# A fused block of four mixers and an expert layer on one NeuronCore: the scan's transposes, GpSimd's pauses and the order of cross attention's output rearranged

## The chip, the cores and the metric

The kernel runs on one core of one Trainium2 chip. It is a single program for a batch of one sequence of 512 tokens with 1024 features, in float32. The metric is the time of one execution on the device in microseconds (us). A core has five engines with queues of their own: PE (matrix multiplications and transposes), DVE (vector work), ACT (activations and scaled copies), POOL (GpSimd: elementwise work, and here the issue of the gathers) and SP (issue of DMAs). They meet only through semaphores.

## The reference, cut to what matters

```python
def peer(h, p):                                   # the expert layer, after cross attention
    q = h @ p["peer_wq"]                          # 8 heads x 2 halves of 128
    s = einsum(q, p["peer_sub_keys"])             # 128 scores for each half
    a, b = top_k(s[first half], 16), top_k(s[second half], 16)
    best, ids = top_k(a[:, None] + b[None, :], 16)      # of 256 sums; id = i * 128 + j
    gates = softmax(best)                         # per head
    u, v = p["peer_u"][ids], p["peer_v"][ids]     # 16 rows of each for a token and head
    return sum(gates * gelu(u . h) * v)
x = x + rmsnorm(mamba2(rmsnorm(x)))               # state space mixer, scan over 4 chunks
x = x + rmsnorm(window_attention(rmsnorm(x)))
x = x + gated_delta_net_and_mlstm(rmsnorm(x))
x = x + cross_attention(rmsnorm(x), memory) @ w_o
x = rmsnorm(x + peer(rmsnorm(x)))
```

(Names are shortened. Every token of the expert layer needs 8 x 16 rows of a table of 16384 rows; `peer_u` and `peer_v` lie beside each other in it, so a row is 8 KB.)

## The kernel before, in words

The 512 tokens are four tiles of 128 (`TT = 4`), and 1024 features are eight blocks of 128 (`DT = 8`). The residual stream `resid` stays on the chip from the first stage to the last.

**Weights.** All dense weights are one stream of units of 128 x 1024. SP loads them into a ring of four (L188). POOL splits each into a high and a low part (`split_weights`, L208 and L211; `split_ahead`, L227 and L229), and PE multiplies in three passes (high x high, high x low, low x high) from two buffers `w_parts`. `w_split` counts split units, and `w_used` the units that PE is done with; a unit may be split when the one two before it has been used. In a product to token tiles (`tokens_out`, L281) a unit serves 4 tiles with 24 matmuls, and 4 units make a chunk of 512 output features.

**Start.** `set_up` issues the four quarters of x, the table of columns, and the first four weight units, and waits for the columns; only after the barrier at its end may `mamba_in` transpose x (L432).

**State space scan.** `mamba_scan` turns 24 blocks of 128 features (96 transposes, L840) through four PSUM banks. DVE copies the even blocks out (L856) and ACT the odd ones (L882). ACT computes the softplus of the time steps after its first four copies (L888 to L891), with two table loads; PE sums the decays only behind the last transpose (L844, L846); then ACT and DVE make the exponentials (L894 to L898, L870, L872), and a barrier follows.

**Output projections.** `NormedOut` (twice: after the scan and after window attention) multiplies by the output weights, scales (L553), sums (L555), adds into `resid` tile by tile (L563), and PE transposes each tile as it is added (L432). The next projection's units are split meanwhile.

**mLSTM.** In `mlstm` DVE works through four chunks (L2378 to L2385), each signalled by `mixed_ready`; POOL multiplies the gate in (L2206) when its chunk is signalled, and scales later (L2209). ACT squares each chunk (L2152) for the norm.

**Cross output and expert layer** (`peer`). `PlainOut` makes chunk 0 and chunk 1 of cross attention's output for all four tiles, adds them (L498), and turns blocks 0 to 3 between the units of chunk 1 and blocks 4 to 7 after it. Then PE computes the queries of the first two columns x = 0, 1 in two halves (L2811: tiles 0 and 1 are "front", 2 and 3 "back", 24 matmuls with 256 columns for each), their scores (L2822), the columns 2 and 3 for all tiles (L2850), and their scores (L2859). DVE picks the best sixteen (`vector_top`, L2665 to L2672), combines two halves of a head and writes the ids (`Choice.vector`, L2730 to L2750). The choice of head 0 is made for tile 0 first, so that gathers can begin, then tile 1. `Choice.vector_gates` needs ACT's exponentials (`Choice.scalar`, L2766). In ACT's queue those of tile 1 stand behind the scores of column 2.

The experts are 512 gathers, each of 128 rows of 8 KB (1.05 MB), issued by POOL (L3078) in a fixed order. Nine buffers are there until gather 207, then thirteen; a gather waits until the row before it in its buffer has been used (`row_used`). For each pair of rows DVE makes the dot products (L3101), ACT the gelu (L3139), DVE the weight (L3093), ACT a diagonal matrix (L3135), and PE adds the weighted rows into PSUM (L3156, four matmul records for a row). Splits of the columns 4 to 15 stand between the gathers in POOL's queue; the first stands ahead of gather 15.

## Time and profile before

| | us |
|---|---|
| median of 3 runs (lowest, highest) | 2681.82 (2678.59, 2682.61) |
| the profiled execution: its own time, and its span | 2678.74, 2677.0 |
| PE busy (share of the span) | 2320.1 (87%) |
| DVE busy | 1568.4 (59%) |
| POOL busy | 1502.8 (56%) |
| ACT busy | 714.9 (27%) |
| DMA queue of the gathers: share of 16 engines' time | 48.3% |

The page of the profile has busy time by engine, the span in 40 slices, and the chain of work that ended last. A share of busy time is a mean over stages with different limits, so the table alone does not say what a change in one stage is worth.

### The profile page before, as it was taken

The numbers are of one execution on the slowest core, as the hardware profiler recorded it, in microseconds if no ns is written. First come the engines' busy times: TensorE is split into PE (matmuls) and PEld (weight loads), VectorE is DVE, ScalarE is ACT, GpSimd is POOL, SyncE is SP. The second block draws the span as 40 slices with busy tenths as digits, with TensorE's granted clock in tenths as the row PEclk, the third lists the DMA queues.
The fourth block names the chain that finished last, engine by engine and source line by source line (L and its number), as shares of the span: only waits on it lengthen the run. The fifth ranks groups of instructions, "written<-read, shape, count | busy, mean of one in ns | idle before, by whom it ended". The sixth has DMA issues, their size and how long they took to land.

```text
span 2677.0 us, 28363 instructions
## 1 busy us (share of the span) xinstructions
PE 2320.1 (87%) x9216; PEld 1519.9 (57%) x9216; DVE 1568.4 (59%) x3381; ACT 714.9 (27%) x1935; POOL 1502.8 (56%) x1060
## 2 busy tenths in 40 slices
PE   8999899899989999789988888888777777777776
PEld 7888678788978879677754443444232223222222
DVE  1266592333431668632387878887778776555555
ACT  2111553214422131423222222222223222111112
POOL 7777377676567754264665656555544444344331
PEclk9999899999989999899999999999999999999999
DMA  4222002222222210031289999999999999999996
GB/s 146 93 95 94 17 1 93 91 100 80 103 88 87 86 63 1 1 110 48 100 339 408 421 421 421 421 413 421 421 422 422 421 421 422 421 422 421 421 421 258
DMA packets 105898, 646.35 MB, mean 241 GB/s; under 512 B 12720, under 2 KB 15152, under 8 KB 39600
## 3 DMA queue, kind: packets, MB, share of 16 engines
q0 software_dynamic: 73728, 536.90, 48.3%
q1 hardware_dynamic: 31776, 106.87, 11.6%
q8 instruction: 65, 1.06, 0.2%
q10 hardware_dynamic: 272, 1.05, 0.1%
q14 instruction: 57, 0.47, 0.0%
HBM read 640.58 MB, written 4.19 MB: 241 GB/s over the span
## 4 chain that ended last, share of the span: by engine, by line
DMA 32%; PE 10%; DVE 5%; POOL 2%; issue 1%; ACT 1%; POOLq 0%; DVEq 0%; ACTq 0%
DMA peer_row<-in_peer_uv,peer_ids 32%; PE bank L3156 7%; DVE peer_row L3101 3%; PE bank L281 2%; POOL peer_row L3078 1%; PE bank L2850 1%; POOL w_parts L229 1%; ACT peer_diag L3135 1%; DVE peer_weight L3093 1%; PE bank L2811 0%; POOL w_parts L227 0%; DVE peer_top_i L2669 0%; DVE peer_picked L2742 0%; DVE peer_sc_left L2672 0%; DVE peer_top_v L2665 0%
## 5 line engine op out<-in xcount | busy, mean ns | idle before, releaser
L3156 PE MATMUL bank<-peer_row,peer_diag 128*128 128x512 f32 x2048 | 966.8, 618 | 266.7 <-ACT peer_diag L3135 264.5
L3078 POOL DMA_INDIRECT peer_row<-in_peer_uv,peer_ids x512 | 585.8, 1144 | 645.6 <-PE bank L3156 604.4
L3156 PEld LDWEIGHTS bank<-peer_row,peer_diag 128*128 128x128 f32 x2048 | 380.0, 194 | 823.5 <-ACT peer_diag L3135 430.0
L3101 DVE CUSTOM_DVE_ANT_0 peer_row<-peer_row,peer_h_tok 128x1024 f32<-128x1024 f32 x512 | 641.0, 1256 | 329.2 <-DMA peer_row<-in_peer_uv,peer_ids 328.3
L208 POOL TENSOR_TENSOR w_parts<-ring,zero 128x1024 fp32r<-128x1024 f32 x156 | 295.5, 1894 | 227.5 <-PE bank L281 112.4
L211 POOL TENSOR_TENSOR w_parts<-ring,w_parts 128x1024 fp32r<-128x1024 f32 x156 | 374.4, 2400 | 29.0 <-POOL w_parts L208 29.0
L3139 ACT ACTIVATE peer_acts<-peer_dots 128x2 f32<-128x2 f32 x256 | 52.1, 204 | 734.0 <-DVE peer_dots L3101 734.0
L3135 ACT ACTIVATE peer_diag<-ident,peer_weight 128x128 f32<-128x128 f32 x512 | 177.5, 394 | 223.8 <-DVE peer_weight L3093 221.1
L257 PE MATMUL bank<-ssm_h_high,w_parts 128*128 128x512 f32 x512 | 157.7, 389 | 0.8 <-DVEq L644 0.8
L257 PEld LDWEIGHTS bank<-ssm_h_high,w_parts 128*128 128x128 f32 x512 | 96.1, 188 | 20.9 <-DVEq L644 1.0
L257 PE MATMUL bank<-hyb_h_high,w_parts 128*128 128x512 f32 x320 | 99.9, 393 | 0.8 <-DVEq L644 0.8
L281 PE MATMUL bank<-w_parts,att_h_high 128*128 128x512 f32 x320 | 98.9, 390 | 1.7 <-DVE att_h_low L442 1.5
L257 PE MATMUL bank<-ssm_h_low,w_parts 128*128 128x512 f32 x256 | 99.6, 389 | 0.0
L2850 PE MATMUL bank<-peer_h_high,w_parts 128*128 128x512 f32 x192 | 86.8, 493 | 0.0
L281 PE MATMUL bank<-w_parts,ssm_h_high 128*128 128x512 f32 x256 | 78.9, 389 | 0.0
L281 PE MATMUL bank<-w_parts,ssm_y_high 128*128 128x512 f32 x256 | 78.8, 389 | 0.0
L3093 DVE TENSOR_TENSOR peer_weight<-peer_acts,peer_gates 128x2 f32<-128x2 f32 x256 | 51.9, 203 | 35.1 <-ACT peer_acts L3139 26.6
L227 POOL TENSOR_TENSOR w_parts<-ring,zero 128x1024 fp32r<-128x1024 f32 x22 | 42.6, 1935 | 49.4 <-ACT xa_p L2573 34.1
L257 PEld LDWEIGHTS bank<-hyb_h_high,w_parts 128*128 128x128 f32 x320 | 60.9, 190 | 13.8 <-DVEq L644 1.0
L281 PEld LDWEIGHTS bank<-w_parts,att_h_high 128*128 128x128 f32 x320 | 59.8, 188 | 14.6 <-issue 1.8
L229 POOL TENSOR_TENSOR w_parts<-ring,w_parts 128x1024 fp32r<-128x1024 f32 x22 | 62.9, 2858 | 1.7
L672 ACT ACTIVATE ssm_conved<-ssm_acc 128x512 f32 x32 | 20.2, 632 | 161.6 <-DVE ssm_acc L661 161.6
(559 smaller groups left out, 3803.8 us busy)
## 6 DMA issues: line engine op xcount, KB each, us to landing
ring<-in_weights SPq DMA_DIRECT2D x180, 512.0 KB, 3.2
peer_row<-in_peer_uv,peer_ids POOLq DMA_INDIRECT x512, 25.4
resid<-in_x SPq DMA_DIRECT2D x4, 512.0 KB, 7.6
out<-resid SPq DMA_DIRECT2D x4, 512.0 KB
xa_mem<-in_mem ACTq DMA_DIRECT2D x1, 1024.0 KB, 4.9
xa_kept<-xa_v_out SPq DMA_DIRECT2D x1, 1024.0 KB
xa_kept<-xa_k_out SPq DMA_DIRECT2D x1, 1024.0 KB
xa_v<-xa_kept SPq DMA_DIRECT2D x1, 1024.0 KB, 5.3
```

The lines of the kernel that those rows point to most:

```text
L208: pool.tensor_tensor(high, m.ring[:, s, :], zeros, ALU.add).then_inc(m.w_high, 1)
L211: pool.tensor_tensor(low, m.ring[:, s, :], high, ALU.subtract).then_inc(m.w_split, 1)
L229: pool.tensor_tensor(low, m.ring[:, u % RING, :], high, ALU.subtract).then_inc(m.w_split, 1)
L257: mm = pe.matmul(out, m.parts[:, s % 2, a, k * P:(k + 1) * P], rhs[b][:, k, :], start=(k == 0 and (a, b) == PASSES[0]), stop=(k == DT - 1 ...
L281: mm = pe.matmul(bank_of(c, t)[:, :], lhs[a][:, k, t * P:(t + 1) * P], m.parts[:, u % 2, b, (k % 2) * 512:(k % 2 + 1) * 512], start=(k == ...
L2850: mm = pe.matmul(self.q_bank(x)[:, :], parts[:, x % 2, a, k * P:(k + 1) * P], self.h[b][:, k, :], start=(k == 0 and (a, b) == PASSES[0]), ...
L3078: pool.indirect_dma_start(self.rows[row][:, :], None, self.m.ins["peer_uv"], bass.IndirectOffsetOnAxis(ap=self.choice.ids[:, t, slot:slot ...
L3093: dve.tensor_tensor(self.weight[:, g % 4, :], self.acts[:, g % 4, :], self.choice.gates[:, t, first:first + GROUP], ALU.mult).then_inc(sel ...
L3101: dot = dve.tensor_tensor_reduce(mine, mine, self.tokens(slot_of(j)[0]), 1.0, 0.0, ALU.mult, ALU.add, self.dots[:, h % 4, r:r + 1])
L3135: act.activation(self.diag[:, j % (2 * GROUP), :], self.m.ident[:, :], ACT.Copy, scale=self.weight[:, g % 4, r:r + 1]).then_inc(self.diag_ ...
L3139: act.activation(self.acts[:, h % 4, :], self.dots[:, h % 4, :], ACT.Gelu).then_inc(self.acts_ready, 1)
L3156: mm = pe.matmul(self.m.banks[2 * t + half][:, :], self.diag[:, j % (2 * GROUP), :], self.rows[row][:, D + half * 512:D + (half + 1) * 512 ...
```

## The change

It edits six places.

1. `set_up` issues only the first quarter of x and the columns and waits for nothing; the other loads are issued at the head of `mamba_in`, and ACT waits for the columns there. The three small rows of `mamba_scan` are loaded in `mamba_in` too.
2. `mamba_scan` turns its blocks through seven banks. DVE takes blocks 0 to 3 and the even ones, ACT the other odd ones. The time steps' chain comes first on DVE and ACT, the sums stand behind block 13, and the exponentials among the last copies.
3. and 4. In the two stages with `NormedOut`, POOL makes the high part of the next projection's first unit, and then pauses until all four tiles have been added. In the second, the small weights are split four units later.
5. In `mlstm`, POOL's gate product of chunk t waits for chunk t + 1.
6. In `peer`, chunk 1 of cross output is made for tiles 0 and 1 first. Four pairs of split weights are held for it. Then come unit 0 of chunk 1 for tiles 2 and 3, the front's transposes, queries and scores, the other three units for tiles 2 and 3, and the back half. The norm is made for each pair of tiles. On DVE the sums of tiles 2 and 3 come after the first choice. Places in memory are changed to fit: the first gather waits until all of cross output's units are used (its buffer lies where the left operand lay), gather 6 until both back halves are done, and gather 8 for the two token tiles.

```diff
@@ split_ahead
+        if pause is not None and u == m.split:
+            pool.wait_ge(*pause)
         pool.tensor_tensor(low, m.ring[:, u % RING, :], high, ALU.subtract).then_inc(m.w_split, 1)
@@ set_up
-            for n in range(4):
-                here = slice(n * D // 4, (n + 1) * D // 4)
-                sp.dma_start(m.resid[:, :, here], x[:, :, here]).then_inc(m.x_loaded[n], 16)
-                if n == 0:
-                    sp.dma_start(m.cols[:, :], m.ins["cols"]).then_inc(loaded, 16)
-                    sp.dma_start(m.ring[:, 0, :], m.ins["weights"][0]).then_inc(m.w_loaded[0], 16)
-            stream_weights(m, sp, RING)
-            sp.wait_ge(loaded, 16)
+            load_tokens(m, sp, 0)
+            sp.dma_start(m.cols[:, :], m.ins["cols"]).then_inc(m.cols_loaded, 16)
@@ mamba_scan
+            SUMS_AFTER, EXPS_AFTER = 13, 15
+            turn_banks = [m.banks[n] for n in (0, 1, 2, 3, 5, 6, 7)]
+            dve_takes = lambda j: j < 4 or j % 2 == 0
                 for j in range(N_TURN):
...
+                    if j == SUMS_AFTER:
+                        pe.wait_ge(dve_dt, 3)
...
@@ mamba_out_attention_in, attention_out_hybrid_in
+            split_ahead(m, pool, RING, pause=(out.added, TT))
@@ HeadNorm.gpsimd
-        pool.wait_ge(self.mixed_ready, t + 1)
+        pool.wait_ge(self.mixed_ready, t + 2)
@@ PairOut (new)
+    def tensor_front(self, pe):
+        for kk in range(4):
+            self.tensor_unit(pe, 0, kk, range(TT))
+        for kk in range(4):
+            self.tensor_unit(pe, 1, kk, (0, 1))
+            if kk < 2:
+                pe.wait_ge(self.added, TT)
+                for k in (2 * kk, 2 * kk + 1):
+                    for t in range(TT):
+                        self.turn.tensor(pe, k, t)
+    def tensor_turn(self, pe, pair):
+        for k in range(4, DT):
+            if k == 4:
+                pe.wait_ge(self.added, TT + 2 * pair + 2)
...
@@ peer, gpsimd
+            out.gpsimd(pool)
+            for x in range(2):
+                queries.gpsimd_split(pool, x, queries.parts, None)
+            for x in range(2, FIRST):
+                queries.gpsimd_split(pool, x, m.parts, queries.u0 - 4 + x - 1)
...
+                if j == 0:
+                    pool.wait_ge(m.w_used, queries.u0)
+                if j == 6:
+                    pool.wait_ge(m.w_used, queries.u0 + 2)
+                if j == 8:
                     pool.wait_ge(tokens_made, 2)
@@ peer, tensor
+            out.tensor_front(pe)
             m.unit += HP
...
+            out.tensor_unit(pe, 1, 0, (2, 3))
+            out.tensor_turn(pe, 0)
+            for x in range(2):
+                queries.tensor_half(pe, x, 0)
+            for x in range(2):
+                queries.tensor_half_scores(pe, x, 0)
+            for kk in range(1, 4):
+                out.tensor_unit(pe, 1, kk, (2, 3))
+            pe.wait_ge(queries.front_read, 2)
+            out.tensor_turn(pe, 1)
...
@@ peer, scalar
             choice.scalar(act, 0, 0, 0, 1)
+            out.scalar_pair(act, 1)
+            for x in range(2):
+                queries.scalar_half_q(act, x, 1)
+            for x in range(2):
+                queries.scalar_half_scores(act, x, 1)
             queries.scalar_q(act, 2)
             queries.scalar_q(act, 3)
             queries.scalar_scores(act, 2)
@@ peer, vector
+            out.vector_first(dve)
+            out.vector_pair(dve, step, 0)
...
             choice.vector(dve, step, 0, 0, 1, alone)
+            for t in range(2, TT):
+                out.add(dve, 1, t)
             dve.wait_ge(gain_loaded, 16)
             dve.wait_ge(rms.ready, 1)
             tokens(0, alone)
+            out.vector_rest(dve, step, 1)
```

## Rows read from the trace of the kernel before

**Rows 1.** The page: DMA share in 40 slices, in tenths, and GB/s.

```profile
DMA  4222002222222210031289999999999999999996
GB/s 146 93 95 94 17 1 93 91 100 80 103 88 87 86 63 1 1 110 48 100 339 408 421 421 421 421 413 421 421 422 422 421 421 422 421 422 421 421 421 258
```

**Rows 2.** Windows: stretch, busy us (and count) by engine, PEclk, DMA share, GB/s.

```profile
1352.00:1353.00 1.00, 1.00 (x7) 0.81 (x6) 1.00 (x2) 0.00 (x0) 1.00 (x1) 1.00 0.00 0
1355.00:1356.00 1.00, 1.00 (x6) 0.83 (x5) 0.88 (x5) 0.00 (x0) 0.70 (x2) 1.00 0.94 385
...
1550.00:1600.00 50.00, 44.47 (x122) 21.71 (x121) 40.69 (x104) 13.85 (x42) 29.74 (x22) 1.00 1.01 421
```

**Rows 3.** Timeline of the start, PE: start, us, engine, line, operation, [idle before].

```profile
9.52 5.21 PE L432 MATMUL bank<-ident,resid 128*128 128x128 f32 x24 [0.90 <-DMA resid<-in_x]
14.48 0.71 PE L281 MATMUL bank<-w_parts,ssm_h_high 128*128 128x512 f32 x2
```

**Rows 4.** Timeline of the scan's transposes: PE, ACT and DVE.

```profile
297.00 6.69 PE L840 MATMUL bank<-ident,ssm_conved 128*128 128x128 f32 x44 [2.68 <-ACT ssm_xs L882]
...
292.66 0.30 ACT L888 ACTIVATE ssm_tmp<-ssm_dt 128x128 f32<-128x128 f32 x1
...
296.36 1.07 ACT L882 ACTIVATE ssm_xs<-bank 128x512 f32<-128x512 f32 x2
...
306.94 0.29 DVE L872 TENSOR_TENSOR ssm_dt_end<-ssm_dt,ssm_dt_end 128x128 f32<-128x128 f32 x1 [0.38 <-ACT ssm_dt_end L898]
```

**Rows 5.** The line L563, first output projection: duration in ns, least, median, most.

```profile
L563 DVE SCALAR_TENSOR_TENSOR resid<-ssm_z_gate,ssm_o_stat,resid x4: 1271/1272/2900, 502.1 to 507.3; 128x1024 f32<-128x1024 f32 x4
```

**Rows 6.** Timeline after the first output projection: POOL and PE.

```profile
501.56 2.34 POOL L211 TENSOR_TENSOR w_parts<-ring,w_parts 128x1024 fp32r<-128x1024 f32 x1 [0.18 <-POOL w_parts L208]
...
505.03 5.80 PE L432 MATMUL bank<-ident,resid 128*128 128x128 f32 x32 [5.73 <-DVE resid L563]
...
512.38 0.70 PE L281 MATMUL bank<-w_parts,att_h_high 128*128 128x512 f32 x2 [1.55 <-DVE att_h_low L442]
```

**Rows 7.** Timeline of mLSTM's end: DVE.

```profile
1131.87 0.16 DVE L2384 TENSOR_TENSOR mls_den<-mls_den,mls_weights 128x4 f32<-128x4 f32 x1
...
1135.47 1.10 DVE L2384 TENSOR_TENSOR mls_den<-mls_den,mls_weights 128x4 f32<-128x4 f32 x1
```

**Rows 8.** The chain that ended last, around the first choice: start, us, what.

```profile
1341.18 5.75 PE bank L2811 x48
...
1348.11 10.91 PE bank L2850 x48
1359.03 2.91 PE bank L2859 x16
...
1364.14 1.22 DVE peer_row L3101
```

**Rows 9.** Timeline, DVE and POOL: the first choice and the gathers 0, 9 and 15.

```profile
1341.21 0.29 DVE L2665 MAX8 peer_top_v<-peer_sc_front 128x8 f32<-128x128 f32 x1 [2.86 <-ACT peer_sc_front L2838]
...
1351.27 1.93 POOL L3078 DMA_INDIRECT peer_row<-in_peer_uv,peer_ids  x1 [6.54 <-DVE peer_ids L2750]
...
1372.83 1.41 POOL L3078 DMA_INDIRECT peer_row<-in_peer_uv,peer_ids  x1 [9.63 <-PE bank L3156]
...
1388.94 1.76 POOL L3078 DMA_INDIRECT peer_row<-in_peer_uv,peer_ids  x1
```

**Rows 10.** Timeline, PE and ACT: column scores, then the first rows.

```profile
1358.87 2.01 PE L2859 MATMUL bank<-peer_keys,peer_q 128*128 128x128 f32 x16
1368.77 11.76 PE L3156 MATMUL bank<-peer_row,peer_diag 128*128 128x512 f32 x22 [7.90 <-ACT peer_diag L3135]
...
1361.96 0.63 ACT L2876 ACTIVATE peer_sc_front<-bank,peer_norm_stat 128x128 f32<-128x128 f32 x2 [2.30 <-PE bank L2859]
...
1364.88 0.63 ACT L2876 ACTIVATE peer_sc_front<-bank,peer_norm_stat 128x128 f32<-128x128 f32 x2 [1.25 <-remote]
```

**Rows 11.** A window around the first rows of the experts, the columns as in rows 2.

```profile
1366.10:1372.90 6.80, 4.13 (x5) 1.85 (x6) 6.28 (x25) 3.02 (x7) 0.07 (x1) 0.50 1.02 428
```

More of the change, by code:

```diff
@@ L217, in split_weights, with split_ahead @@
         four(i, u0, False)
-def split_ahead(m, pool, n, parts=None):
+def split_ahead(m, pool, n, parts=None, pause=None):
     for u in range(m.split, m.split + n):
@@ L782, in _ @@
         def _(act):
+            act.wait_ge(m.cols_loaded, 16)
             for k in range(DT):
@@ L2789, in __init__, with gpsimd_split @@
         self.u0 = m.unit + DT
-        self.parts = m.at(58, "peer_parts", [P, 2, 2, UNIT], F32R)
+        self.parts = m.at(74, "peer_parts", [P, 2, 2, UNIT], F32R)
+    def gpsimd_split(self, pool, x, parts, used):
+        m, u = self.m, self.u0 + x
+        high, low = (parts[:, x % 2, n, :] for n in range(2))
+        pool.wait_ge(m.w_loaded[u % RING], 16 * (u // RING + 1))
+        if used is not None:
+            pool.wait_ge(m.w_used, used)
+        pool.tensor_tensor(high, m.ring[:, u % RING, :], m.zero[:, :].broadcast_to([P, UNIT]), ALU.add).then_inc(m.w_high, 1)
+        pool.wait_ge(m.w_high, u + 1)
+        pool.tensor_tensor(low, m.ring[:, u % RING, :], high, ALU.subtract).then_inc(m.w_split, 1)
+        m.split += 1
     def q_bank(self, x):
```

238 lines of the change are left out of this document (165 added, 73 removed).

## The prediction

> **What bounds the kernel now.** I read the page first, for where the DMA engines are full. From slice 20 on they move 408 to 422 GB/s [rows 1], and a stretch in the middle of the experts shows 1.01 of their time busy with PE at 44.47 of 50 us [rows 2]. That is a hard floor: 512 gathers of 1.05 MB at 421 GB/s are 2.49 us each, 1275 us, and no engine's saving shortens them. So the time has two parts. Ahead of the first gather it is set by PE and by the handovers at which PE waits; there a microsecond saved is a microsecond. Behind it, it is set by when the stream of gathers begins to flow and whether it ever dries up. I then read the timelines at each place that the diff touches [rows 3 to 7], the chain of waits across the first choice [rows 8], and the timeline of the gathers [rows 9].
>
> How the stream begins decides the last part. The first gather is issued at 1351.27 [rows 9]; in 1352 to 1353 nothing moves, in 1355 to 1356 it is 385 GB/s [rows 2], and a ramp between them puts the first bytes at about 1353.9, so 2.6 us after the issue. Nine buffers hold nine gathers, which last until 1353.9 + about 0.7 (ramp) + 9 x 2.49 = 1377.0. The tenth can be issued only when PE has used the first row: 1372.83, bytes from 1375.4. So the stream survives with 1.6 us to spare. An earlier first gather is worth its gain only if the tenth comes earlier too.
>
> **Start: 0.** PE's quarter-one transposes begin at 9.52 on the arrival of x, and the first product at 14.48 [rows 3]. The barrier that falls away let PE begin earlier, but the later quarters come in the same saturated byte stream, the last blocks still wait for them, and their issues now stand behind the barrier. I take 0; from 1.5 gained (the first quarter's blocks out of the way) to 1.0 lost (the issues of one load after another, later).
>
> **Scan: -6.4.** Before, PE waits 2.68 us for a bank [rows 4], since ACT makes the softplus from 292.66 on and takes a bank out only from 296.36, 3.7 us. Behind the last transpose (297.00 + 6.69 = 303.7) come sums, exponentials and table load until 306.94 + 0.29 = 307.23, a tail of 3.5. After, seven banks with DVE on blocks 0 to 3 cover the softplus, and the tail's work lies beside transposes 13 to 23. Walking the 96 transposes at 0.15 us each (6.69 / 44) with the copies at 0.54 (1.07 / 2) dealt between two engines, the last copy ends at about 300.85 instead of 307.23: 2.68 less in the stall, 3.5 less in the tail and 0.2 in the copies. Range -7.5 to -4.5: the lower end if a bank is short once for some 2 us.
>
> **Pauses: -4.1.** The first of four L563 takes 2.900 us, the others 1.27 [rows 5]. POOL's low part runs from 501.56 for 2.34 us [rows 6], so to 503.90; the add began at 502.1 and ends 1.27 behind 503.7 at 505.0, where PE's wait of 5.73 us ends. With the pause that add takes 1.27: 1.63 less. The small reduction ahead of it, which stands beside POOL's high part, gives about 0.4 more (an estimate: the small operation in [rows 7] shows 1.10 beside POOL and 0.16 alone). So 2.05; the second projection has the same pattern once more (its first add at 792.1), so 4.1 in all. What the pause costs: the low part now begins after the four adds, about 4.5 us later, and each unit behind it comes about that much later. PE needs it at about 510.4 (512.38 less 2.0 [rows 6]) and it would be done at about 509.2; the cover is PE's 5.80 us of transposes and the split of that one block in DVE and ACT. If that cover were gone, up to 1 us comes back: range -4.8 to -3.0.
>
> The Trainium skill, page "SBUF — State Buffer", section "Who interferes with whom", says that a DVE instruction with two SBUF inputs and a GpSimd instruction that reads SBUF share one port pair, and that the first to issue holds it for its whole length. The trace agrees (2.900 beside 1.27). By that rule the change also pays somewhere: it moves the splits of columns 0 to 2 beside the first choice, where DVE's pair sums read SBUF twice.
>
> **mLSTM: -0.5.** L2384 takes 1.10 beside POOL's product and 0.16 alone [rows 7]; in two of the chunks' steps it is on the way. But the product moved a chunk later stands beside other small operations. From -1.3 to +0.3.
>
> **Peer: +4.5.** Ahead of the choice PE no longer makes three units of chunk 1 for tiles 2 and 3. These are 3 x 12 matmuls at 0.227 (10.91 / 48 [rows 8]), 8.2; blocks 4 to 7 of two tiles, 8 transposes at 0.15, 1.2; and about 0.6 for a norm and copies of half the tiles. So the first MAX8 comes 10.0 earlier, at about 1331.2 instead of 1341.21 [rows 9]. POOL's split of the third column falls on DVE's pair sums (the stretch of up to 1.6 seen in [rows 5]): +1.4 (10.0 - 1.4 = 8.6). So ids and first gather are 8.6 earlier, at about 1342.7. The wait on w_used for that gather's place is met by then: PE finishes the three units at about 1339.4.
>
> But the rest of the stage is longer. DVE adds tiles 2 and 3 only after the choice, so PE has nothing from 1339.4 to 1343.6, about 4 us, then transposes to 1345.4. I expect the granted clock to fall there: where PE had been idle 7.90 us ahead of 1368.77 [rows 10] the window 1366.1 to 1372.9 shows 0.50 [rows 11], the lower level of 1.2 GHz, against 1.00 in the middle. The back halves are 5.75 at full clock [rows 8]; with some 2.1 lost at the low one and a queue of transposes they end near 1352.4, their scores at 1353.6, and the columns, 10.91 long [rows 8], at 1364.5, where before they ended at 1359.04. That is 5.5 later, and everything behind it hangs on it in ACT's order: two scores, the exponentials of tile 1, the gates, the first dot at 1364.14 + 5.5 = 1369.6. DVE has nothing between about 1358 and 1369.5. The tenth gather moves with it: 1372.83 + 5.5 = 1378.3, bytes from 1380.9. The nine gathers, though, are over at 1377.0 - 8.6 = 1368.4. The stream resumes 1380.9 - 1377.0 = 3.9 later than it would have had to, so of the 8.6 gained nothing remains. Add 0.6 for the sixteenth gather, which stands behind a split at 1388.94 [rows 9] with about 1.5 us to spare: +4.5. Range +1.5 (clock not lost, back halves early) to +9 (clock low through both back halves and rows used later).
>
> The page "TensorE: Matmul & The Clock Gate", section "HAM oscillation — how this bites in real kernels", says that waits of PE inside a loop bring its clock back to half and are paid each time. By it the idle PE ahead of the back transposes would cost as counted; this trace agrees in [rows 11]. Both pages are of the Trainium skill.
>
> **The sum.** 0 - 6.4 - 4.1 - 0.5 + 4.5 = -6.5. The profiled execution took 2678.74 with a span of 2677.0; so a span of 2670.5 and a time of 2672.2. The median of the three runs lies 3.08 above the profiled one, so 2675.3 on that scale. With all ends together the change is -13.6 to +2.8.
>
> **Rivals.** R1: the earlier gathers count in full, because the rows are used as early (the ids alone drive them). Then -11.0 - 8.6 = -19.6, 2662.2. For it: the first gather is 8.6 earlier. Against: it needs the tenth at 1364, and the dots wait for ACT's exponentials, which stand behind two columns of PE work. R2: the peer stage costs 9, from low clock through both back halves (5.75 more) and gathers waiting later: -11.0 + 9 = -2, 2679.8, no change. For it: [rows 11]; against: PE has dense work behind its wait. R3, the other side: while gathers flow, handovers from PE to ACT come late. Before, the first eight of the scores' matmuls that start at 1358.87 end near 1359.9, but ACT begins at 1361.96 [rows 10], 2.0 late, and the chain books 2.91 where PE's records fill 2.01 [rows 8, 10]; the last end at 1360.88 and ACT begins at 1364.88, in the very stretch where the stream begins. After the change five more handovers (two half queries, two half scores, the first column) lie behind the first gather: at 2.0 to 2.9 each 10 to 14.5, so -6.5 + 10 to 14.5 = +3.5 to +8, about 2687; it is slower beyond 2.4 each. Against: others beside them come in time. R4: the change doesn't do what it says in the scan, since one engine's copies bound the rest: -4.6 + 4.5, about 0, 2681.7.
>
> **How the numbers follow.** Forecast 0.60 (-10 to -3), R1 0.06, R2 0.22, R3 0.04, R4 0.08. A measurement of this kernel tells 0.2%, 5.4 us. Faster by more: R1 and 0.52 of the forecast's cases, 0.58; slower: R3, 0.04; same 0.38. The range, 2668.5 to 2681.5, leaves out R1, R3 and about 0.1 at the edges; the forecast's own is 2671.8 to 2678.8.
>
> **What would show it.** Start: the first L281 at 14.5. Scan: no PE wait over 1 us inside L840, L872 ended by about 300.9. Pauses: all eight L563 at 1.27, and the product behind them without a longer wait. mLSTM: L2384 at 0.16. Peer, on the time of before less 11: the first MAX8 10 earlier, the first gather 8.6 earlier, a PE wait of about 4 us ahead of the back transposes and a granted clock near 0.5 after it, DVE idle for about 11 us ahead of the first L3101, that one 5.5 later, and GB/s near zero for some 12 us between the ninth and the tenth gather. No such gap, and R1 is right; a first dot more than 10 later, R2; ACT starting over 2 us behind PE's ends, R3. The step most likely wrong is the tenth gather, which a low clock or an earlier row moves one for one.

## The result and the profile after

| | before | after |
|---|---|---|
| median, us (lowest, highest) | 2680.39 (2678.59, 2682.61), 5 runs | 2667.02 (2665.44, 2669.28), 5 runs |
| the profiled execution: own time, span | 2678.74, 2677.0 | 2667.02, 2665.3 |

The change makes the kernel faster by 0.5%: ratio 0.995, 95% interval 0.9935 to 0.9964, so 9.6 to 17.4 us, 13.4 by the medians. Forecast were 2675.3 and a range of 2668.5 to 2681.5. The direction is right, the size is double, and the time lies 1.5 us below the range. The forecast stood on the 2681.82 that the kernel before had after three runs; five put it at 2680.39. So of the 8.3 us between 2675.3 and 2667.02, 1.4 are the base and 6.9 the change: 13.4 instead of 6.5.

From here on lines are named as the kernel after numbers them: L851 (L840 before) are the scan's transposes, L880 its last step, L972 the first product behind it, L566 the four adds of an output projection (L563), L435 the transposes behind them (L432), L2396 mLSTM's small product (L2384), L3250 the gathers, L3273 the dots, L3328 the weighted rows.

First the floor. In the page of the kernel after, GB/s in 40 slices is as in [rows 1]: full from slice 21 on, counted from 0. (The prediction reads slice 20 as full; it has 339 GB/s before and 337 after.)

```profile
GB/s 147 93 97 94 16 17 87 95 95 81 104 80 95 95 48 1 22 103 35 132 337 411 421 421 421 421 417 421 421 422 422 421 421 421 421 422 421 421 421 259
```

The start and the scan in its timeline (start, us, engine, line):

```profile
13.63 0.96 PE L284 MATMUL bank<-w_parts,ssm_h_high 128*128 128x512 f32 x2
...
286.24 7.97 PE L851 MATMUL bank<-ident,ssm_conved 128*128 128x128 f32 x56 [1.15 <-PEq L723]
...
294.49 4.53 PE L851 MATMUL bank<-ident,ssm_conved 128*128 128x128 f32 x40
301.37 1.12 PE L972 MATMUL bank<-ssm_cut,after 128*128 128x512 f32 x2 [2.34 <-ACT ssm_cut L1007]
...
299.23 0.28 DVE L880 TENSOR_TENSOR ssm_dt_end<-ssm_dt,ssm_dt_end 128x128 f32<-128x128 f32 x1
```

The first product begins 0.85 earlier than in [rows 3]; by the scan 0.54 of it is left. The wait of 2.68 inside the transposes [rows 4] is gone, and the last step ends at 299.51 instead of 307.23, 7.7 earlier. But PE's first product behind the barrier shows something else. In the kernel before it is this row:

```profile
309.09 2.08 PE L962 MATMUL bank<-ssm_cut,after 128*128 128x512 f32 x2 [4.96 <-ACT ssm_cut L997]
```

PE had been idle for 4.96 us there, and the two matmuls took 2.08; after the change it is idle for 2.34, and they take 1.12. That is TensorE's clock: the windows of before (columns as in [rows 2]; the last but two is the granted clock) show it at half, 1.2 GHz, behind the barrier.

```profile
301.10:308.00 6.90, 3.03 (x27) 2.84 (x26) 2.66 (x5) 4.65 (x10) 0.24 (x1) 0.99 0.00 0
308.00:315.00 7.00, 5.91 (x17) 3.85 (x17) 1.97 (x4) 5.63 (x18) 6.69 (x12) 0.52 0.00 0
```

Some 6 us further on the kernel after is 10.1 us ahead (DVE's first sum behind the products, at 305.59 instead of 315.66), and not 7.7. The forecast had no term for this.

The output projections (the line L566 with its least, median and most ns; then the timeline):

```profile
L566 DVE SCALAR_TENSOR_TENSOR resid<-ssm_z_gate,ssm_o_stat,resid x4: 1279/1280/1286, 492.1 to 495.7; 128x1024 f32<-128x1024 f32 x4
L566 DVE SCALAR_TENSOR_TENSOR resid<-att_qk,att_o_stat,resid x4: 1279/1279/1285, 781.1 to 784.7; 128x1024 f32<-128x1024 f32 x4
```

```profile
493.40 6.35 PE L435 MATMUL bank<-ident,resid 128*128 128x128 f32 x32 [3.67 <-DVE resid L566]
...
501.31 0.70 PE L284 MATMUL bank<-w_parts,att_h_high 128*128 128x512 f32 x2 [1.55 <-DVE att_h_low L445]
...
782.40 5.24 PE L435 MATMUL bank<-ident,resid 128*128 128x128 f32 x32 [3.68 <-DVE resid L566]
```

No add is held up any more, and PE waits 3.67 and 3.68 instead of 5.73 [rows 6]: 2.06 each, as costed. The product behind still waits 1.55 for DVE and for no split, so the pause is covered. From the transposes' start to the next product it is 7.91 us at the first place instead of 7.35, and 6.79 at the second instead of 7.40: the clock again, once against and once for the change. mLSTM's L2396 is at 606 ns in the mean instead of 885 (lines of each kernel in 1100 to 1150, mean of four):

```profile
L2396 DVE TENSOR_TENSOR mls_den<-mls_den,mls_weights 128x4 f32<-128x4 f32 x4 | 2.4, 606 | 0.1
```

```profile
L2384 DVE TENSOR_TENSOR mls_den<-mls_den,mls_weights 128x4 f32<-128x4 f32 x4 | 3.5, 885 | 0.1
```

How far the kernel after is ahead, by the start of the same instruction in the two timelines:

| | before | after | ahead |
|---|---|---|---|
| first product | 14.48 | 13.63 | 0.85 |
| scan, DVE's first sum behind the products | 315.66 | 305.59 | 10.07 |
| first product of window attention | 512.38 | 501.31 | 11.07 |
| first product behind window attention | 802.46 | 789.19 | 13.27 |
| DVE's first step of the convolution there (L657, L658) | 879.14 | 864.28 | 14.86 |
| transposes behind mLSTM | 1145.52 | 1127.91 | 17.61 |
| first product of cross attention's output | 1285.96 | 1270.97 | 14.99 |
| end of the span | 2677.0 | 2665.3 | 11.7 |

Between the last two places ahead of the expert layer 2.6 us are lost, 2.5 of them in cross attention, whose code is the same. Its last products (L2499, L2511) follow the same waits of 2.95 and 0.69 us, and took 7.13 before and 9.18 after:

```profile
1276.32 7.13 PE L2499 MATMUL bank<-xa_pt,xa_v 128*128 128x512 f32 x16 [0.69 <-ACT xa_pt L2580]
```

```profile
1259.30 9.18 PE L2511 MATMUL bank<-xa_pt,xa_v 128*128 128x512 f32 x16 [0.69 <-ACT xa_pt L2592]
```

It is the profile before that is the odd one: of the seventeen others, sixteen lose 1.4 to 3.0 us to half clock there. So the new order starts with 15.0 us in hand and ends with 11.7: cross attention's output and the expert layer cost 3.3 in this pair. Their timeline, DVE and PE, then POOL:

```profile
1310.77 2.20 DVE L2795 TENSOR_TENSOR peer_norm_stat<-peer_norm_sums 128x2 f32<-128x2 f32 x1
...
1316.28 0.29 DVE L2677 MAX8 peer_top_v<-peer_sc_front 128x8 f32<-128x128 f32 x1 [2.90 <-ACT peer_sc_front L2986]
...
1319.69 1.63 DVE L2742 TENSOR_TENSOR peer_cand<-peer_top_v 128x256 f32<-128x256 f32 x1
...
1353.73 0.16 DVE L2768 RECIPROCAL peer_total<-peer_total 128x1 f32<-128x1 f32 x1 [10.48 <-ACT peer_gates L2778]
...
1354.13 1.22 DVE L3273 CUSTOM_DVE_ANT_0 peer_row<-peer_row,peer_h_tok 128x1024 f32<-128x1024 f32 x1
...
1328.59 1.94 PE L2865 MATMUL bank<-ident,resid 128*128 128x128 f32 x8 [4.15 <-DVE resid L2871]
...
1358.77 7.65 PE L3328 MATMUL bank<-peer_row,peer_diag 128*128 128x512 f32 x13 [7.18 <-ACT peer_diag L3307]
```

```profile
1328.19 1.15 POOL L3250 DMA_INDIRECT peer_row<-in_peer_uv,peer_ids  x1 [4.60 <-DVE peer_ids L2762]
...
1362.82 1.06 POOL L3250 DMA_INDIRECT peer_row<-in_peer_uv,peer_ids  x1 [21.29 <-PE bank L3328]
```

Windows of the same kernel, the last two columns being DMA share and GB/s:

```profile
1348.00:1352.00 4.00, 3.59 (x24) 3.13 (x22) 0.00 (x0) 1.90 (x7) 0.00 (x0) 1.00 1.01 422
1352.00:1356.00 4.00, 0.00 (x0) 0.00 (x0) 2.20 (x5) 3.92 (x8) 0.00 (x0) 0.95 0.29 117
1356.00:1360.00 4.00, 1.23 (x2) 0.71 (x3) 3.93 (x16) 0.90 (x3) 0.00 (x0) 0.50 0.01 2
1360.00:1364.00 4.00, 4.00 (x7) 1.60 (x7) 3.82 (x12) 0.90 (x3) 1.06 (x1) 0.70 0.00 0
1364.00:1368.00 4.00, 4.00 (x11) 1.74 (x10) 3.93 (x16) 0.90 (x3) 2.62 (x2) 1.00 0.88 293
```

The forecast's picture is all there: the first gather is 23.1 earlier than in [rows 9], the tenth only 10.0, and between them the engines of the DMA stand still for about 11 us. Counted from the first product of cross attention's output, the first MAX8 is 9.9 earlier, the first gather 8.1 earlier, the first dot 5.0 later and the tenth gather 5.0 later; forecast were 10.0, 8.6, 5.5 and 5.5. Behind PE's wait of 4.15 us the clock is at half as expected:

```profile
1328.50:1331.00 2.50, 2.42 (x12) 2.45 (x13) 2.50 (x3) 2.43 (x8) 2.19 (x2) 0.50 0.40 85
```

### The profile page after: what moved, and what is told of

Same layout as the page of the kernel before. It is cut to its first block, busy times and chain, and to the rows that moved or that the text cites. A ratio compares the mean times of both kernels' runs of the same rounds, so it can differ in the third digit from the quotient of the medians.

```text
span 2665.3 us, 28354 instructions
## 1 busy us (share of the span) xinstructions
PE 2319.4 (87%) x9216; PEld 1519.7 (57%) x9216; DVE 1567.2 (59%) x3390; ACT 716.9 (27%) x1940; POOL 1507.0 (57%) x1060
## 4 chain that ended last, share of the span: by engine, by line
DMA 32%; PE 11%; DVE 5%; POOL 2%; issue 1%; ACT 1%; POOLq 0%; DVEq 0%; ACTq 0%
DMA peer_row<-in_peer_uv,peer_ids 32%; PE bank L3328 7%; DVE peer_row L3273 2%; PE bank L2837 1%; PE bank L2997 1%; POOL peer_row L3250 1%; POOL w_parts L232 1%; ACT peer_diag L3307 1%; DVE peer_weight L3265 1%; PE bank L2959 0%; POOL w_parts L228 0%; DVE peer_top_i L2681 0%; DVE peer_place L2681 0%; DVE peer_top_v L2677 0%; DVE peer_sc_left L2684 0%
## 5 line engine op out<-in xcount | busy, mean ns | idle before, releaser
L3328 PE MATMUL bank<-peer_row,peer_diag 128*128 128x512 f32 x2048 | 969.0, 620 | 262.2 <-ACT peer_diag L3307 260.7
L3250 POOL DMA_INDIRECT peer_row<-in_peer_uv,peer_ids x512 | 591.0, 1154 | 652.0 <-PE bank L3328 611.5
L3328 PEld LDWEIGHTS bank<-peer_row,peer_diag 128*128 128x128 f32 x2048 | 382.4, 195 | 819.1 <-ACT peer_diag L3307 418.5
L3273 DVE CUSTOM_DVE_ANT_0 peer_row<-peer_row,peer_h_tok 128x1024 f32<-128x1024 f32 x512 | 645.8, 1266 | 325.6 <-DMA peer_row<-in_peer_uv,peer_ids 325.0
L209 POOL TENSOR_TENSOR w_parts<-ring,zero 128x1024 fp32r<-128x1024 f32 x148 | 280.3, 1894 | 191.7 <-PE bank L260 84.3
L212 POOL TENSOR_TENSOR w_parts<-ring,w_parts 128x1024 fp32r<-128x1024 f32 x148 | 354.5, 2395 | 27.6 <-POOL w_parts L209 27.6
L2997 PE MATMUL bank<-peer_h_high,w_parts 128*128 128x512 f32 x224 | 96.9, 478 | 0.0
L232 POOL TENSOR_TENSOR w_parts<-ring,w_parts 128x1024 fp32r<-128x1024 f32 x22 | 63.1, 2867 | 23.1 <-DVE resid L566 21.5
L228 POOL TENSOR_TENSOR w_parts<-ring,zero 128x1024 fp32r<-128x1024 f32 x22 | 42.4, 1927 | 44.1 <-ACT xa_p L2585 34.1
```

Of the source, the lines that this page charges most:

```text
L209: pool.tensor_tensor(high, m.ring[:, s, :], zeros, ALU.add).then_inc(m.w_high, 1)
L212: pool.tensor_tensor(low, m.ring[:, s, :], high, ALU.subtract).then_inc(m.w_split, 1)
L232: pool.tensor_tensor(low, m.ring[:, u % RING, :], high, ALU.subtract).then_inc(m.w_split, 1)
L2997: mm = pe.matmul(self.q_bank(x)[:, :], m.parts[:, x % 2, a, k * P:(k + 1) * P], self.h[b][:, k, :], start=(k == 0 and (a, b) == PASSES[0]) ...
L3250: pool.indirect_dma_start(self.rows[row][:, :], None, self.m.ins["peer_uv"], bass.IndirectOffsetOnAxis(ap=self.choice.ids[:, t, slot:slot ...
L3273: dot = dve.tensor_tensor_reduce(mine, mine, self.tokens(slot_of(j)[0]), 1.0, 0.0, ALU.mult, ALU.add, self.dots[:, h % 4, r:r + 1])
```

## The experiments

All were timed beside the kernel before; a gain is given from the ratio to it, with its 95% interval, and medians are in us. The kernel before had medians of 2679.16 to 2680.44 in these series.

### The parts alone

The diffs are those of the change, part by part.

Parts 1 to 5 without part 6:

> The kernel before with the edits ahead of the expert layer (start, scan, both pauses, mLSTM) and with the old order of cross output. Theory A (from the trace after: everything up to the end of mLSTM stands 17.6 us earlier, and the expert layer gives 5.9 of it back): 17.6 us faster than before, and faster than the changed kernel by about 6. Rival B (the expert layer's new order gave the extra gain, and the 17.6 is swallowed by the stream of gathers whatever the order): 11 to 12 faster, the same as the changed kernel.

Median 2664.35, ratio 0.9944 (0.993 to 0.9957): 15.0 faster, and 2.7 faster than the changed kernel by the medians, which the two intervals don't tell apart. First gather at 1334.57, tenth at 1356.16. Theory A's 17.6 was read ahead of cross attention; the 15.0 us at the layer's first product fit the measured 15.0. The interval touches rival B's 11 to 12 at its lower end, so this run alone doesn't rule it out; part 6 alone does.

Part 6 alone:

> The kernel before with the new order of cross output and the expert layer alone. Theory A: 5 to 6 us slower than before, with the first gather about 5.5 earlier, the first dot product about 7.6 later, and the DMA engines idle for about 10 us between the ninth and the tenth gather. Rival B: not slower, up to 3 faster.

Median 2683.95, ratio 1.0021 (1.0012 to 1.003): 3 to 8 us slower, 5.6 by the ratio. First gather 1341.72 (9.6 earlier than [rows 9]), first dot 1368.08 (3.9 later), tenth gather 1376.77 (3.9 later); this profile is 1.45 ahead at the layer's first product (1284.51 instead of 1285.96) for no reason in its code, so set against that the gather is 8.1 earlier and the dot and the tenth gather 5.4 later, close to the forecast of 8.6 and 5.5. The change's largest part, by itself, costs.

Parts 1 and 2:

> The kernel before with the edits at the start and in the scan alone. Theory A (order and clock: 0.5 at the start, 7.2 in the order of the scan's work, and 2.3 more because PE is idle for 2.3 instead of 5.0 us ahead of the first cut product and keeps the granted clock of 1.0): 9.5 to 10 faster, and the first L972 record near 1.12 us instead of 2.08. Rival B (order alone): 7 to 8 faster, with the first cut products at 2.08 as before.

Median 2671.80, ratio 0.9974 (0.9964 to 0.9985): 7.0 faster. In its trace the first product behind the barrier is as in the changed kernel:

```profile
300.21 1.13 PE L970 MATMUL bank<-ssm_cut,after 128*128 128x512 f32 x2 [2.34 <-ACT ssm_cut L1005]
```

It is 10.3 us ahead where the first output projection's products begin (401.65 instead of 411.97), but the span is only 7.3 shorter: 1.6 us are lost in mLSTM and 1.7 in cross attention, where no code differs. Theory A is right at the place; the time is nearer to rival B's 7 to 8, and the interval, 4.0 to 9.6, reaches to both.

Parts 3 and 4:

> The kernel before with GpSimd's pauses in the two output projections alone. Theory A (2.05 us at each from the shared port; what more or less is seen is the granted clock behind each wait, which differs with where the waits fall): between 3 and 6 faster, with the four adds at 1.27 us each and PE's wait ahead of the transposes 3.7 instead of 5.7. Rival B (the later split of the small weights is what gave the extra 1.2 us seen around 872): the stretch at 871.9 to 874.5 runs at full clock here too and the gain is 5 to 6 each time.

Median 2673.92, ratio 0.9975 (0.9965 to 0.9985): 6.7 faster, 4.0 to 9.4. Each of PE's waits is 3.67 or 3.68. And the stretch named by rival B does run at full clock here, some 50 us behind the last instruction that was moved (the split of the small weights, at 812.65); first the windows of before, then of this kernel:

```profile
868.00:872.00 4.00, 2.38 (x13) 1.96 (x13) 0.69 (x1) 0.69 (x1) 3.64 (x2) 0.90 0.40 131
872.00:876.00 4.00, 4.00 (x14) 3.14 (x13) 0.00 (x0) 0.00 (x0) 0.63 (x1) 0.68 0.40 131
```

```profile
864.00:868.00 4.00, 3.16 (x16) 2.51 (x16) 0.69 (x1) 0.00 (x0) 3.05 (x2) 1.00 0.18 69
868.00:872.00 4.00, 4.00 (x19) 3.29 (x19) 0.70 (x1) 0.00 (x0) 0.67 (x1) 1.00 0.37 131
```

PE does the same in both (two waits of 0.8 us), and no wait was removed there. It isn't chance either: in all thirteen profiles with the pauses this stretch is at full clock and 1.6 us are gained by 879, in all five without them half clock follows for 3.4 us. Whether the pauses do it or the later split of the small weights, which this kernel also has, was not separated; rival B's sign came true.

Part 5:

> The kernel before with the later gate product of mLSTM alone. Theory A (the port's stretch of L2384 only): 0.5 to 1.5 faster, L2384 at 0.16 throughout. Rival B (no change, the product now collides with other small operations): 0.

Median 2676.69, ratio 0.9989 (0.998 to 0.9998): 0.5 to 5.4 faster. L2384 is at 420 ns in the mean, not at 0.16 throughout: three of the four are, and the first, 1.19 us long, stands beside another product of GpSimd's (L2200), which the edit leaves alone. DVE is 0.9 further ahead behind the third of them, which took 1.10 before. The measurement can't place the gain any closer.

### The clock behind a wait

Before, with PE's wait in the scan filled:

```diff
+                for _w in range(18):
+                    pe.transpose(m.banks[7][:, 0:P], m.ident[:, :], m.ident[:, :])
```

> The kernel before with 18 more transposes of the identity into an unused bank behind the scan's sums, where PE would wait (about 3 us of the wait of 5.0). Theory A (the granted clock behind the barrier is a cost of its own, paid because PE is idle for 5.0 us): PE's first cut products take 1.1 instead of 2.1 us, the clock is 1.0 from 308 on, and the kernel is about 2 faster than before, though it does more work. Rival B (the clock falls whatever PE does there): no change, or slower by the added work.

```profile
302.31 2.13 PE L849 MATMUL bank<-ident 128*128 128x128 f32 x18
307.44 1.12 PE L964 MATMUL bank<-ssm_cut,after 128*128 128x512 f32 x2 [3.00 <-ACT ssm_cut L999]
```

The products are at 1.12: theory A holds at the place, where the kernel comes to stand 2.3 further ahead within 5 us. But the median is 2679.98, ratio 1.0002 (0.9993 to 1.0011). In its profile the gain is lost again in cross attention, where 1271 to 1289 shows a clock of 0.72, and the same work in the kernel before (1273 to 1291) 1.00:

```profile
1271.00:1289.00 18.00, 14.50 (x30) 7.56 (x31) 4.90 (x8) 3.47 (x6) 4.49 (x4) 0.72 0.14 49
```

```profile
1273.00:1291.00 18.00, 12.83 (x42) 7.61 (x43) 6.59 (x8) 3.47 (x6) 6.17 (x4) 1.00 0.16 59
```

But there the profile before is the exception, as said above, so this pair doesn't tell where the gain went. Ahead of 1295 us this profile has as much time at half clock as the one before, 68.3 us, though it has none behind the barrier. The gain of 2.3 that was seen at the place lies just outside the interval (at most 1.9 faster).

The other way: the changed kernel with the wait made long again by work that nobody needs.

```diff
+                for _w in range(6):
+                    step(act.activation(cut[:, 0, 0, :], m.upto[:, :], ACT.Copy, scale=a[:, 0, 0:1]))
                 make_cut(0)
```

> The changed kernel with six more small copies on ACT ahead of the first cut in the scan, some 2 to 2.5 us, so that PE waits there for about 4.5 to 5 us as in the kernel before. Theory A (a longer wait costs its length and the clock behind it): the first cut products at 2.1 us instead of 1.1, the scan's products 4.5 to 5 later than in the changed kernel though only 2 to 2.5 was added. Rival B (length alone): 2 to 2.5 later, products at 1.1.

```profile
302.76 2.07 PE L972 MATMUL bank<-ssm_cut,after 128*128 128x512 f32 x2 [4.94 <-ACT ssm_cut L1007]
...
298.83 2.57 ACT L1012 ACTIVATE ssm_cut<-upto,ssm_a 128x128 f32<-128x128 f32 x6 [0.38 <-PEq L824]
```

2.57 us of ACT's work bring back 2.07 for the products. Ahead of the wait this profile is 1.21 earlier than the changed kernel's, behind the products 2.55 later: 3.8 for 2.6 of wait, near theory A's lower end. At the place the wait costs its length and about half as much again. Median 2671.52, ratio 0.9971 (0.9961 to 0.9981): 4.5 slower than the changed kernel by the medians. That the total pays for the clock too is not shown: an interval this wide doesn't tell 4.5 from 2.6, and in the profile the lead was made up elsewhere, down to 0.8 us at the layer's first product (1271.73 instead of 1270.97); the rest of its longer span lies behind that.

Of the eighteen profiles, all five in which PE waits there for 4.94 to 4.96 us have the products at 2.07 or 2.08, and all thirteen in which it waits for 2.34 or 3.00 have them at 1.12 or 1.13.

The changed kernel with three more waits filled (20, 20 and 22 transposes of the identity ahead of L435, twice, and L2865):

> The changed kernel with 20 transposes of the identity ahead of the transposes in both output projections and 22 ahead of the back half's (PE would wait 3.7, 3.7 and 4.15 us there). Theory A (clock behind a wait is a cost at each place and the sum of these is what is left): transposes behind all three at 1.0, 1 to 3 us faster than the changed kernel. Rival B (as with the filled wait in the scan: the local stretch is quicker by some 2 us, but the granted clock falls at other places later, and the median stays): within 1 us of the changed kernel.

Both output projections' transposes take 4.68 instead of 6.35 and 5.24, but at the layer's first product this profile is only 0.1 us ahead of the changed kernel's (1270.86 instead of 1270.97). Median 2665.41, ratio 0.994 (0.9926 to 0.9953): 1.6 better than the changed kernel, inside what can be told.

### Where the expert layer's gain went

The changed kernel with its first gather held back:

```diff
                 if j == 0:
                     pool.wait_ge(m.w_used, queries.u0)
+                    pool.wait_ge(out.pair_ready, 8)
```

> The changed kernel with the first gather held back until DVE has made the low parts of the back half, about 4.3 us (issue near 1332.5 instead of 1328.2). Theory A (the nine gathers end at 1354.7 and the tenth comes at 1364.6, so the first has 10 us to spare): no change in time, tenth gather at 1362.8 as before, the gap in the bytes 4 us shorter. Rival B (the first gather's time counts): 4 slower.

In this profile everything ahead of the layer is 5.3 us earlier, so the ids are ready at 1321.96, and the gather is issued at 1328.05, 6.1 behind them instead of 0.9. The tenth comes at 1357.82, 5.0 earlier: it moved with the rest and not with the first. Median 2665.44, ratio 0.9949 (0.9936 to 0.9962), the same as the changed kernel's 0.995. Five us of delay cost nothing that can be measured. The times alone would not exclude rival B's 4, which lies within the two intervals together; the trace speaks for theory A, since the tenth gather comes as late in the layer as in the changed kernel (92.1 us behind its first product, and 91.9 there). (Its span is only 2.1 shorter, so the layer is 3.2 longer than in the changed kernel's profile. Part 6 alone, with the same order and nothing held back, has it 3.5 longer, so this isn't the delay's doing.)

ACT's exponentials of the second choice ahead of the columns:

```diff
+            choice.scalar(act, 1, 0, 1, 1)
             queries.scalar_q(act, 2)
             queries.scalar_q(act, 3)
             queries.scalar_scores(act, 2)
-            choice.scalar(act, 1, 0, 1, 1)
```

> The changed kernel with one call moved: ACT makes the exponentials of tile 1's first choice before the copies of columns 2 and 3 instead of behind the first of their scores. Theory A (DVE, idle for 10.5 us ahead of the first dot, waits for this alone, but PE's rows still stand behind the column scores): first dot product about 1343.5 instead of 1354.1, first weighted row on PE about 1356 instead of 1358.8, tenth gather about 3 to 4.5 us earlier, and the kernel 3 to 4.5 faster than the changed one. Rival B (the tenth gather depends on PE's column work alone): first dot early, tenth gather and time unchanged.

```profile
1342.79 1.22 DVE L3273 CUSTOM_DVE_ANT_0 peer_row<-peer_row,peer_h_tok 128x1024 f32<-128x1024 f32 x1
...
1354.32 7.97 PE L3328 MATMUL bank<-peer_row,peer_diag 128*128 128x512 f32 x14 [3.53 <-ACT peer_diag L3307]
...
1358.00 1.44 POOL L3250 DMA_INDIRECT peer_row<-in_peer_uv,peer_ids  x1 [17.36 <-PE bank L3328]
```

The first dot is 11.3 earlier, the weighted rows 4.5, the tenth gather 4.8, and 0.9 of each lies ahead of the layer. Median 2664.24, ratio 0.9945 (0.9931 to 0.9958): 2.8 better than the changed kernel, within the noise of one comparison. The trace has theory A's order of events.

DVE's sums of tiles 2 and 3 inside the first choice (a callback between its steps adds both tiles, and the loop behind `choice.vector` goes):

> The changed kernel with DVE's two sums of cross output for tiles 2 and 3 inside the first choice (ahead of its id part, where PE has just finished them) instead of behind it. Theory A (the late sums hold PE for 4.15 us and, through it, columns, scores and the tenth gather): ids and first gather 1.3 later, PE's back half about 2.8 earlier, tenth gather 2.5 to 3.5 earlier and the kernel as much faster than the changed one. Rival B (the first gather counts): 1.3 slower.

```profile
1325.23 1.06 PE L2865 MATMUL bank<-ident,resid 128*128 128x128 f32 x8 [1.58 <-DVE resid L2871]
...
1330.50 0.39 PE L2959 MATMUL bank<-peer_h_high,peer_parts 128*128 128x256 f32 x1 [2.78 <-DVE peer_h_low L2888]
```

PE's wait is 1.58 instead of 4.15, and a new one of 2.78 stands behind the transposes, for the low parts, which DVE makes behind two token tiles. The sum is the same, the tenth gather at 1362.28, the median 2666.70, ratio 0.9953 (0.9939 to 0.9966). My theory was wrong by the next wait in DVE's queue.

Both moves:

> Both moves. Theory A (they act on the same chain, one on its ACT piece and one on its PE piece, and so add): tenth gather 6 to 7.5 us earlier than in the changed kernel, 6 to 7 faster than it, about 18 to 20 faster than before. Rival B (the stream's floor is reached sooner): 3 to 4 faster than the changed kernel.

Median 2661.88, ratio 0.9932 (0.9918 to 0.9945), tenth gather at 1357.82. Between the theories: 5.1 better than the changed kernel by the medians. The tenth gather is 5.0 earlier, of which the exponentials alone had 4.8; the sums add nothing to speak of.

The first pair of rows ahead of the scores as well:

```diff
             for x in range(2, FIRST):
                 queries.tensor_column(pe, x, range(DT))
+            for h in range(2):
+                experts.tensor(pe)
             for x in range(2, FIRST):
                 queries.tensor_scores(pe, x)
-            for h in range(STEPS):
+            for h in range(2, STEPS):
```

(With the exponentials early, ACT makes the first gelu ahead of `scalar_q(2)` and the first diagonals ahead of `scalar_q(3)`; DVE makes two pairs' dots ahead of its loop.)

> The changed kernel with the exponentials moved as in the run before, and the first pair of expert rows pulled ahead: DVE makes the first two pairs' dot products and the first weights before the top of column 2, ACT the first gelu and diagonals between the copies of columns 2 and 3, PE the first pair's weighted rows ahead of the scores of columns 2 and 3. Theory A (what is given back in the expert layer is the drying up of the gathers, since the tenth waits for a row that stands behind columns and scores): tenth gather issued near 1351.5 instead of 1358.0, no gap in the DMA's bytes after 1354, and 5 to 6 us faster than with the exponentials alone, 22 to 24 faster than before. Rival B (the gap only moves, to the next gathers or to the sixteenth, behind its split): gather ten early, but the time 0 to 2 better.

```profile
1350.57 0.94 POOL L3256 DMA_INDIRECT peer_row<-in_peer_uv,peer_ids  x1 [10.39 <-PE bank L3334]
1352.29 0.94 POOL L3256 DMA_INDIRECT peer_row<-in_peer_uv,peer_ids  x1 [0.78 <-PE bank L3334]
1358.72 0.94 POOL L3256 DMA_INDIRECT peer_row<-in_peer_uv,peer_ids  x1 [5.49 <-PE bank L3334]
```

```profile
1350.00:1354.00 4.00, 3.80 (x21) 2.51 (x19) 0.00 (x0) 1.05 (x5) 1.87 (x2) 1.00 0.93 363
1354.00:1358.00 4.00, 1.54 (x4) 0.82 (x5) 3.81 (x14) 1.81 (x7) 0.00 (x0) 1.00 0.97 350
1358.00:1362.00 4.00, 4.00 (x11) 1.54 (x10) 3.82 (x14) 0.94 (x4) 2.08 (x2) 1.00 0.65 211
```

The long gap is gone: the tenth gather is 12.3 earlier than in the changed kernel, and what is left is a share of 0.65 where the twelfth waits for the second pair. Median 2659.77, ratio 0.9928 (0.9915 to 0.9942): 19.3 faster than before, 7.3 faster than the changed kernel by the medians. Between A and B: a part of the gap moved to the later gathers.

The same with DVE's sums early and the token tiles behind the low parts:

> As the run before, and DVE adds tiles 2 and 3 inside the first choice and makes the low parts of the back half ahead of the two token tiles. Theory A (with the late sums alone the wait only moved from the transposes to the low parts behind the token tiles, 2.78 us): PE's back half starts 2.5 to 3 us earlier, tenth gather near 1349, and as the stream no longer dries up the gain is that of the first gather alone: 0 to 1 better or 1 worse. Rival B (the back half still sets the stream): 2.5 to 3 better.

Median 2661.32, ratio 0.9924 (0.991 to 0.9938): no difference from the run before. The tenth gather is issued at 1352.32 and not near 1349; from the layer's first product it is as late as in the run before. The layer's own wait of PE is not what sets the stream any more.

The second pair ahead of the scores too, and that kernel with both projections' waits filled:

> As the run with the first pair of rows pulled ahead, with the second pair too: PE makes both pairs ahead of the scores of columns 2 and 3. Theory A (what is left of the gap, 0.65 of DMA share in 1358 to 1362, is the twelfth gather behind the scores): twelfth gather issued near 1355.5 instead of 1358.7, share 1.0 there, 1 to 2 faster than with the first pair alone. Rival B (the scores' delay comes back at the choice of the next head): same or slower.

> The run beside it, and PE's waits in both output projections filled with 20 transposes of the identity each. Theory A (their clock behind it is a cost): another 0.5 to 2 faster. Rival B: within 1 of it.

Medians 2660.47, ratio 0.9926 (0.9914 to 0.9939), and 2662.14, ratio 0.9936 (0.9922 to 0.9949). The twelfth gather is issued at 1356.51, but in 1366 to 1370 the DMA share is 0.60 and in 1374 to 1378 0.61: the hole only moved, to the fourteenth gather, whose rows stand behind the scores now, and to the sixteenth. Neither is better than one pair. The kernel with one pair ahead is the fastest by its median, and the measurement doesn't tell it from these three.

## Why the prediction was wrong, step by step

- **Start, 0.** 0.85 at the first product, 0.54 by the scan. Right within its range.
- **Scan, -6.4 (to -7.5).** The order of the work alone gave 7.2 (7.7 less the start's 0.5); with the clock behind the barrier, 9.5 locally (10.1 less 0.5). Timed alone with the start, 7.0 (4.0 to 9.6). The term was right within its range for what it costed, and left out the 2.3 of the clock.
- **Pauses, -4.1 (to -4.8).** The port's share is exact: 2.06 at each place, all eight adds at 1.28. The clock behind the two waits took 0.6 at one place and gave 0.6 at the other. The 1.6 us near 872, there in every profile with the pauses, had no term. Timed alone the part gave 6.7 (4.0 to 9.4), which doesn't exclude 4.1.
- **mLSTM, -0.5 (to -1.3).** 0.9 on DVE in its own profile, for the operation that the term named. Timed alone 2.9, with 0.5 to 5.4.
- **Together** the forecast had -11.0 ahead of the expert layer; measured were 15.0 (11.5 to 18.8) without part 6, 15.0 at the layer's first product in the profile after, and 16.6 as the sum of the parts.
- **Peer, +4.5.** Timed alone +5.6 (3.2 to 8.0), in the profile after +3.3. The mechanism stood as written, and so did its numbers: late sums, idle PE, half clock behind it, first dot and tenth gather 5.0 late for 5.5, a dry stream. The first gather came 8.1 earlier for 8.6. GpSimd's split held DVE twice and not once (L2795 took 2.20 besides L2742's 1.63), and the gather was issued 0.65 later behind the ids than before; neither mattered much, since the held-back gather shows no price for a later first one. The stream's fresh start was about 1 us quicker than in [rows 9].

The step that failed is the sum ahead of the expert layer, 11.0 instead of 15.0: I wrote each saved wait at its own length, and charged the granted clock in the peer stage only. In its place the runs show two amounts of clock that come with the change in every profile: 2.3 us behind the scan's barrier, where eighteen profiles of eighteen tell the clock by the wait, and 1.6 us near 872, thirteen of thirteen against none of five. At the barrier the stretched wait shows a price of 3.8 for 2.6, and the change's own wait, 2.6 shorter, gave 4.9 (2.6 and 2.3). The remaining places up to the layer, the order in the scan (0.8 more than forecast), the start (0.5), mLSTM and the stretches where no code differs, gain and lose against each other in this pair.

Adding up the time that each profile's granted clock shows at 1.2 GHz ahead of 1295 us gives 68 to 75 us in the four kernels with the old scan and the old projections, 58 in each of the two with one of them changed, and 41 to 61 in the twelve with both. The kernel after has 54.6, the one before 68.3; PE does half as much in it, so the 13.7 are worth up to 6.8 us, more than the 4.0 to be explained.

What stays open is the exact share. Of one and the same code up to the layer there are eight profiles, and at the layer's first product they stand 13.7 to 20.2 us ahead of the kernel before: a difference of up to 6.6 without any edit, and the last has 17.0 us less of half clock up to there than the first. Filling one wait in the kernel before, or three in the changed one, moved the local time and not the median by anything that can be told. So the price at the places is shown, and that the total pays it is supported by the time without part 6 and by the three groups of profiles, but not shown by any single wait.

The Trainium skill's page "TensorE: Matmul & The Clock Gate", section "HAM oscillation — how this bites in real kernels", says of a loop in which PE waits for data that the waits bring the clock to half and that the price is paid at each. By that rule the scan's barrier and both projections would have had a term of their own. These runs agree where a wait was stretched; where one was filled, they agree at the place and not in the total; and at the scan's barrier the waits of 2.3 to 3.0 us were not charged at all.

R1 (the earlier gathers count in full) gave 2662.2 and is refuted, though the result lies nearer to it than to 2675.3: it needed an earlier tenth gather, and that one is 5.0 later in the layer; part 6 alone is slower; and the first gather held back by five us changed nothing. R2 (a first dot more than 10 later), R3 and R4 didn't happen; ACT's scores follow PE's ends here by 0.3 us.

## What to carry to other kernels

When a wait of PE gets shorter, cost two things: its length, and the clock of the work behind it, read from windows on either side of the wait; and do it for every wait that the change touches, not only for those that it adds. Take that as the price at the place: whether the total pays it, only timed runs tell, and here filled waits didn't. Before you take a lead from two profiles, compare it in a stretch whose code is the same in both. A stream with a fixed number of buffers starts when its first buffer comes back, not when its first transfer is issued, so ask what frees the first buffer before paying for an earlier issue; here moving one ACT call and one pair of rows gave 7.3 us by the medians, where the whole reordering cost 5.6. When you move an operation forward in one engine's queue, read what that engine does next for the same consumer: the wait may only change its name.

## What the runs showed of the hardware

- The same two PE waits of 0.78 and 0.84 us near 868 were followed by 3.4 us of half clock in five kernels of five and by full clock in thirteen of thirteen. The granted clock depends on more than the work just ahead of it in program order.
- A stream of gathers that had run dry was soon full again: behind the tenth, issued at 1362.82, the three us from 1364 on show 115, 229 and 426 GB/s. Behind the first gather of the kernel before, issued at 1351.27, the three from 1353 on show 66, 172 and 385.
- A DVE sum of 128 x 2 numbers took 2.20 us beside GpSimd's split, more than a sum of 256 columns (1.63) beside the same kind of work. It began 0.22 behind GpSimd's low part (1310.55, 2.40 us) and ended with it at 1312.95 to 1312.97: here the price was what was left of GpSimd's instruction, not the size of DVE's.
